# Re-placing the state-space table steps and the spatial gate's loads in a hand-written schedule

## The reference, cut to what matters

```
h = rms_norm(x, pre_g);  a_u, a_v, a_g, b_x, b_g, x_q, x_g, gates = split(h @ w_in)
y_a = a_u * (causal w_s @ layer_norm(a_v) + b_s) * silu(a_g)          # spatial gate
y_b = s5(b_x) * silu(b_g)                                             # state space
y_x = attention(x_q, rms_norm(mem) @ wk, rms_norm(mem) @ wv) * silu(x_g)
out = x + rms_norm((sum_n sigmoid(gates_n) * (y_n @ w_branch_n)) @ w_out, post_g)
```

## Time and profile before

| what | value |
|---|---|
| median of 3 runs | 2296.23 us (2295.5 to 2297.37) |
| the profiled execution: its own time | 2300.16 us |
| its span, first to last instruction | 2298.4 us |
| mean granted clock of TensorE | 0.994 of full speed |
| PE busy | 2258.7 us, 98% |
| PE weight loads (beside PE) | 1957.5 us, 85% |
| DVE busy | 1762.1 us, 77% |
| ACT busy | 1027.1 us, 45% |
| POOL busy | 298.0 us, 13% |
| device memory | 206 GB/s over the span |

### The profile page before, as it was taken

How to read it: one execution, slowest core, us unless ns; L and a number is a source line. 1 busy time by engine, 2 the same in 40 slices (tenths; PEclk the granted TensorE clock), 3 DMA queues, 4 the chain that set the end, 5 groups by cost and what they waited for, 6 DMA issues and landing times.

```text
span 2298.4 us, 30093 instructions
## 1 busy us (share of the span) xinstructions
PE 2258.7 (98%) x12660; PEld 1957.5 (85%) x12660; DVE 1762.1 (77%) x1974; ACT 1027.1 (45%) x850; POOL 298.0 (13%) x226
## 2 busy tenths in 40 slices
PE   8999999999999999999999999899999999999998
PEld 7988888888888888888888888788888888888886
DVE  7595568657797898787766889979999968458865
ACT  5553335334444545445444435344444444544432
POOL 0002200210000000000000000045887500000000
PEclk9999999999999999999999999999999999999999
DMA  7443454347755555555555566566666687576754
GB/s 271 147 159 138 147 200 153 140 147 258 276 201 201 202 201 220 202 203 202 205 205 206 204 222 227 185 244 214 210 210 212 210 294 256 192 243 250 264 205 146
DMA packets 84230, 475.19 MB, mean 207 GB/s; under 512 B 8704, under 2 KB 8832, under 8 KB 32512
## 3 DMA queue, kind: packets, MB, share of 16 engines
q1 hardware_dynamic: 84096, 473.27, 58.1%
HBM read 450.17 MB, written 23.07 MB: 206 GB/s over the span
## 4 chain that ended last, share of the span: by engine, by line
PE 84%; DVE 11%; DMA 2%; issue 1%; ACT 1%; DVEq 0%; SPq 0%; ACTq 0%
PE acc L2180 26%; PE acc L2183 25%; PE acc L2186 25%; DVE w_lo L1263 4%; PE banks L2327 2%; PE banks L2376 1%; DMA raw<-in_w 1%; DVE a_raw L1310 1%; DVE convT L1583 1%; DVE padT L1310 1%; PE banks L2455 1%; ACT w_hi L803 1%; DMA spilled<-stage 1%; PE banks L2197 1%; DVE stats L1377 0%
## 5 line engine op out<-in xcount | busy, mean ns | idle before, releaser
L1263 DVE TENSOR_TENSOR w_lo<-raw,w_hi 128x2048 fp32r<-128x2048 f32 x394 | 912.4, 2318 | 352.7 <-ACT w_hi L803 349.7
L803 ACT ACTIVATE w_hi<-raw 128x2048 fp32r<-128x2048 f32 x394 | 751.2, 1912 | 630.8 <-DMA raw<-in_w 630.2
L2180 PE MATMUL acc<-w_hi,a_hi 128*128 128x512 f32 x2112 | 815.1, 386 | 14.5 <-DVE w_lo L1263 9.4
L2183 PE MATMUL acc<-w_lo,a_hi 128*128 128x512 f32 x2112 | 802.7, 380 | 0.0
L2186 PE MATMUL acc<-w_hi,a_lo 128*128 128x512 f32 x2112 | 802.2, 380 | 0.0
L2180 PEld LDWEIGHTS acc<-w_hi,a_hi 128*128 128x128 f32 x2112 | 400.3, 190 | 84.7 <-issue 13.4
L2186 PEld LDWEIGHTS acc<-w_hi,a_lo 128*128 128x128 f32 x2112 | 400.4, 190 | 57.5 <-DVE a_lo L1299 0.3
L2183 PEld LDWEIGHTS acc<-w_lo,a_hi 128*128 128x128 f32 x2112 | 400.5, 190 | 54.0
L2180 PE MATMUL acc<-w_hi,b_hi 128*128 128x512 f32 x928 | 352.3, 380 | 0.0
L2183 PE MATMUL acc<-w_lo,b_hi 128*128 128x512 f32 x928 | 351.7, 379 | 0.0
L2186 PE MATMUL acc<-w_hi,b_lo 128*128 128x512 f32 x928 | 351.7, 379 | 0.0
(11 more groups left out here) (351 smaller groups left out, 1680.6 us busy)
## 6 DMA issues: line engine op xcount, KB each, us to landing
raw<-in_w SPq DMA_DIRECT2D x395, 1024.0 KB, 4.8
spilled<-stage SPq DMA_DIRECT2D x72, 256.0 KB, 5.9
gate_in<-spilled SPq DMA_DIRECT2D x20, 512.0 KB, 5.8
x_rows<-in_x SPq DMA_DIRECT2D x4, 512.0 KB, 9.1
x_rows<-in_x SPq DMA_DIRECT2D x1, 2048.0 KB, 10.3
mem_rows<-in_mem SPq DMA_DIRECT2D x2, 1024.0 KB, 5.9
spilled<-stage_b SPq DMA_DIRECT2D x8, 256.0 KB, 5.8
out<-y_rows SPq DMA_DIRECT2D x3, 512.0 KB, 2.8
```

The lines of the kernel that those rows point to most:

```text
L803: act.activation(w_hi[:, n % HIGH, :], raw[:, n % RAW, :], ACT.Copy)\
L1263: dve.tensor_tensor(w_lo[:, n % RAW, :], raw[:, n % RAW, :], w_hi[:, n % HIGH, :].bitcast(F32), ALU.subtract).then_inc(lo_split, 1)
L2180: pe.matmul(o, hi[:, tk], wh, start=first, stop=False)
L2183: pe.matmul(o, hi[:, tk], wl, start=False, stop=False)
```

## The change

It edits only `schedule()` and divides two steps. (1) `ssm_small` 0 goes from slot 242 to the start of slot 247, 1 from the end of slot 244 to place 497 (the end of slot 248). What stood in part 1 is now in four parts (1, 11, 12, 13) and what stood in part 2 in two (2, 14), one at the end of each of the slots 248 to 253, parts 3 to 10 before the split of slots 254 to 261. (2) ACT's exp, tanh and sines are a step `ssm_sin` of their own, at the start of slot 248. (3) The loads of c are issued two slots earlier, in slot 245. (4) `ssm` starts 2 slots later, with all that is placed relative to it: `load_av` is now at slot 321, and a of the cross attention is 335 and not 333. `xa_gate` is placed relative to `w2_gate2` and stays at slot 349. (5) From `load_av` on, the loads of the spatial gate are two slots apart (321, 322, 324, 326, 328), `sg_norm` stands at places 648, 650, 652, and ACT's square root (`sg_root`) at place 649, behind the split.

```diff
-    put(end("xa_wv", 1) + 2, "ssm_small", 0)
-    put(end("xa_wv", 1) + 4, "ssm_small", 1)
-    for part in range(2, 11):
-        put_at(2 * end("xa_wk", 1) - 2 + 2 * part, "ssm_small", part)
-    put(end("xa_wk", 1) - 1, "load_c")
+    at = 2 * end("xa_wk", 1) - 2
+    put_at(at + 2, "ssm_sin")
+    for place, part in ((0, 0), (3, 1), (5, 11), (7, 12), (9, 13), (11, 2), (13, 14)):
+        put_at(at + place, "ssm_small", part)
+    for part in range(3, 11):
+        put_at(at + 8 + 2 * part, "ssm_small", part)
+    put(end("xa_wk", 1) - 3, "load_c")
     a = end("w2_bx", 1) + 1
...
-        at = 2 * (a + 3) + 1 + SSM_PLACES * i
+        at = 2 * (a + 5) + 1 + SSM_PLACES * i
...
-    a += 3 + -(-SSM_PLACES * 17 // 2)
-    for i, name in enumerate(("load_av", "load_ln_gb", "load_au", "load_ag")):
-        put(a - 1 + i, name)
-    put(a + 4, "load_km")
+    a += 5 + -(-SSM_PLACES * 17 // 2)
+    for place, name in ((-1, "load_av"), (0, "load_ln_gb"), (2, "load_au"), (4, "load_ag"), (6, "load_km")):
+        put(a + place, name)
+    put_at(2 * a + 5, "sg_root")
...
             def ssm_small(part):
+                if part:
+                    return
+                act.wait_ge(pe_used, end(f"w_mlp_down{NPIECE - 1}", 3))
+                act.activation(ssm_t[:, 0, :], cols["log_dt"], ACT.Exp).then_inc(act_done, me.done("ssm.dt"))
+
+            def ssm_sin():
                 T_ = lambda i: ssm_t[:, i, :]
...
+                act.wait_ge(dve_done, me.at("ssm.ab"))
+                act.activation(T_(4), T_(1), ACT.Exp).then_inc(act_done, me.done())
+                act.activation(T_(5), T_(1), ACT.Tanh, scale=0.5).then_inc(act_done, me.done())
+                act.activation(T_(6), T_(3), ACT.Sin).then_inc(act_done, me.done())
+                act.activation(T_(7), T_(3), ACT.Sin, scale=0.5).then_inc(act_done, me.done("ssm.sin"))
...
-
-
+                if part == 11:
...
+                if part == 12:
...
+                if part == 13:
...
+                if part == 14:
...
-                if part >= 3:
+                if 3 <= part <= 10:
```

More of the change, by code:

```diff
@@ L1021, in ssm_small @@
             def ssm_small(part):
-                T_ = lambda i: ssm_t[:, i, :]
[L1023 to L1031, removed]
+                if part:
[3 more added lines that the diff above has]
+            def ssm_sin():
+                T_ = lambda i: ssm_t[:, i, :]
+                act.wait_ge(dve_done, me.at("ssm.ab"))
[3 more added lines that the diff above has]
+                act.activation(T_(7), T_(3), ACT.Sin, scale=0.5).then_inc(act_done, me.done("ssm.sin"))
             def ssm_u():
@@ L1098, in _ @@
                      "hidden_square": hidden_square,
-                     "ssm_small": ssm_small, "ssm_u": ssm_u, "ssm_gelu": ssm_gelu,
-                     "sg_norm": lambda part: root("sgn", 64, NT) if part == 0 else None,
+                     "ssm_small": ssm_small, "ssm_sin": ssm_sin, "ssm_u": ssm_u, "ssm_gelu": ssm_gelu,
+                     "sg_root": lambda: root("sgn", 64, NT),
                      "gelu_turn": gelu_turn, "plain_hi": plain_hi,
```

## The result

| kernel | us, median (lowest to highest) | runs | ratio to before, 95% |
|---|---|---|---|
| before | 2295.5 (2294.84 to 2297.37) | 5 | |
| changed | 2305.69 (2304.6 to 2306.48) | 5 | 1.0043 [1.0028, 1.0057] |
| before, beside the last experiments | 2296.88 (2293.61 to 2300.17) | 23 | |
| changed, timed again with them | 2303.93 (2301.07 to 2305.22) | 6 | 1.0029 [1.0017, 1.0041] |

The changed kernel is slower, by 10.2 us in the first timing and by 7.1 us in the second. The forecast was 2302.6 us (range 2296.5 to 2309), from +6.4 us between profiled executions. Those two took 2300.16 and 2306.13 us: +6.0.

The account below looks back on a forecast made before the run. PE, busy 98% of the span, was taken as the bound, so only its idle and lower clock count. Terms -8.4 - 1.6 + 16.4 + 0 = +6.4 us gave 2306.6 profiled, 2302.6 us at the median (range 2296.5 to 2309).

Parts of the forecast that it names:

- tables (244 to 255): Ahead of units 247 and 251: 12.6 us of idle and lower clock go, 4.2 us come at unit 250; net 8.4 won.
- gate and state space (256 to 351): Spatial gate's 1.6 us of PE waits all won; state space stage priced at nothing.
- late load (351 to the end): load_xg stuck behind unit 351, splits queued behind xa_gate: 14.2 us idle plus 2.2 us lower clock, 16.4 us lost.
- My +4.5 by that rule: Whole sum if the skill's transfer rule priced xg_rows' two loads at 4.4 us, making the late idle 1.8 us shorter.
- The new idle: PE idle ahead of unit 250, from ssm_sin ahead of ACT's split: 2.5 us, plus 1.7 us of lower clock.
- The spatial gate: Loads two slots apart and the root no longer holding a split back win 1.6 us; bound: none of it.
- The state space stage: DVE waits up to 4 us for POOL's first rotation in slot 262; price nothing, bound 2 us lost.
- The early gains: Rival one, units 244 to 255: all 14.2 us won, late stall at its lower bound; +1.2, 2297.4 us; chance 0.26.
- The load is not hidden: Denies rival two: load_xg lands early enough for unit 352's split, faster, 2286 us; chance 0.08.
- the third rival: Denser state space stage starves PE by 2 us, late load costs 17.9: +10.5, 2306.7 us; chance 0.14.

Follow-up runs that it names:

- Experiments 2 to 5: Late stall: load_xg earlier and xa_gate later (ratio 0.9967), attention later in the kernel before (1.0069), only the load earlier (0.9997), only xa_gate later (0.9986).
- experiment 2: Changed kernel with load_xg one slot earlier and xa_gate two slots later: 2287.4 us, ratio to before 0.9967.
- Experiments 9 to 11: Repaired kernel with gate loads bunched: 2284.61 us; with the old root place as well: 2284.8 us; kernel before with only the spatial gate's edits: 2296.01 us.
- the repaired kernel: Changed kernel with load_xg one slot earlier, xa_gate two slots later and ssm_sin half a slot later, behind ACT's split of unit 250: 2283.13 us, ratio 0.9943.
- run 3: Kernel before with a of the cross attention 335 instead of 333, xa_gate still at slot 349: 2311.2 us, ratio 1.0069.
- experiments 4 and 5: Changed kernel with only load_xg one slot earlier: 2295.33 us, ratio 0.9997; with only xa_gate two slots later: 2293.78 us, ratio 0.9986.

## Why the prediction held, and where it did not

The direction and the term that decides it were right; one smaller term, the step to the median that hangs on it, and one reason were not. The stretches of the trace answer to the terms of the sum:

```
                                predicted   first profiles   all profiles
tables (244 to 255)                -8.4         -8.4            -7.4
gate and state space (256 to 351)  -1.6         -1.9            -2.0
late load (351 to the end)        +16.4        +16.9           +17.0
start (to unit 243)                 0           -0.7          scatter
```

"All profiles" takes means: 73.56 us for five profiles with the old tables against 66.21 for five with the new ones and the sines in front; 551.45 (three) against 549.44 (ten); 245.28 (three) against 262.27 (four). The start ranges from 1422.2 to 1426.6 us over all 14 profiles, 1424.5 in the mean, with no order by kernel.

**The late load**, the term that decides the sign, came as worked out. Here are SP's queue in the changed kernel, beside the earlier trace rows, the landing of xg_rows, beside the earlier trace rows, and DVE, beside the earlier trace rows:

```profile
2042.86 0.90 SPq L752 DMA_DIRECT2D spilled<-stage  x2
2043.93 1.33 SPq L645 DMA_DIRECT2D xg_rows<-spilled  x2
```

```profile
DMA to landing us min/median/max: 6.8/7.1/7.3
```

```profile
1456.98 2.29 DVE L1267 TENSOR_TENSOR w_lo<-raw,w_hi 128x2048 fp32r<-128x2048 f32 x1 [4.96 <-ACT w_hi L805]
...
1536.08 1.23 DVE L1923 TENSOR_TENSOR prod<-banks,rot 128x1024 f32<-128x1024 f32 x1 [3.65 <-POOL rot L1228]
...
2052.20 2.29 DVE L2018 TENSOR_TENSOR xqT<-xqT,xg_rows 128x2048 f32<-128x2048 f32 x1 [21.69 <-DMA xg_rows<-spilled]
2054.41 6.69 DVE L1267 TENSOR_TENSOR w_lo<-raw,w_hi 128x2048 fp32r<-128x2048 f32 x3
```

From the end of unit 351 (2042.1) the store's issues end after 1.7 us, where I had 2.45; the loads land at 2052.2, 6.8 to 7.3 us after their issue, at the upper end of my 6.2 to 7.2; `xa_gate` takes 2.2 us, and PE restarts 2.44 us after the split begins. These small errors partly cancel, which is luck: 14.73 us of idle, where I took 14.2 from 13.7 to 14.7. The clock behind it costs 16.86 - 14.73 = 2.1 us (predicted 2.2). Experiments 2 to 5 show cause and shares.

The landing bears on a rule. The same two loads took 3.7 to 4.5 us in experiment 2, issued ahead of the store at a DMA share of 0.77 (2035 to 2040). They took 5.0 to 6.2 us in the kernel before, also ahead of the store, at a share of 0.94 (2036 to 2045), and 6.8 to 7.3 in the changed one, behind the store, at 0.99 (2043 to 2052). The Trainium skill, "DMA: Bandwidth & Descriptors", Anatomy of one DMA, gives 2.0 us plus bytes / 436e3 for a transfer (for GpSimd's path; these are SP's); taken as one transfer of 1 MB, the two loads would take an estimated 4.4 us by it. The trace agrees with that in the first case and not in the others. (My +4.5 by that rule starts from 6.2 us; from the 6.7 us that my 14.2 goes by, it would be +4.1.) What goes with the time here is how full the DMA engines are, more than the place against the store; no run here varied that share by itself.

**The tables.** The new idle came as worked out too: 2.53 us against 2.5. ACT's timeline answers to the earlier trace rows:

```profile
1451.62 0.20 ACT L870 ACTIVATE stats<-stats 128x2 f32<-128x2 f32 x1 [2.49 <-DVE stats L1401]
1451.84 1.28 ACT L1032 ACT_TABLE_LOAD   x1
1453.14 0.23 ACT L1032 ACTIVATE ssm_t<-ssm_t 128x32 f32<-128x32 f32 x1
1453.27 0.21 ACT L1033 ACTIVATE ssm_t<-ssm_t 128x32 f32<-128x32 f32 x1
1453.50 1.28 ACT L1034 ACT_TABLE_LOAD   x1
1454.80 0.23 ACT L1034 ACTIVATE ssm_t<-ssm_t 128x32 f32<-128x32 f32 x1
1454.93 0.21 ACT L1035 ACTIVATE ssm_t<-ssm_t 128x32 f32<-128x32 f32 x1
1455.05 5.49 ACT L805 ACTIVATE w_hi<-raw 128x2048 fp32r<-128x2048 f32 x3
```

From the root's end, 1451.82, to the split at 1455.05 are 3.23 us; I had 3.2. The idle that the change removes is there in every profile with the old tables (5.26 to 5.28 us at the first stop, 1.95 to 2.79 at the second). What the prediction had wrong here was the lower clock behind the old stops, 3.2 + 1.7 us from a single execution. The five profiles have 5.2, 2.3, 2.1, 4.9 and 4.6 us in all, so the mean is 3.8, and the term is -7.4 instead of -8.4.

The same rows show what the load of a table costs: the two at 1451.84 and 1453.50 begin 0.02 us after the instruction ahead of them ends, last 1.28 us, and the next instruction begins 0.02 us after their end. The Trainium skill, "ScalarE: Activation LUTs", What ACT_TABLE_LOAD costs, adds 1.38 us of drain to each; an estimate by it has 2.8 us more of idle, 5.3 in all. The trace has 2.53, so it does not bear the drain out here.

**The spatial gate.** Size right (-1.9 against -1.6), reason wrong. The prediction said that the spaced loads and the root behind the split win it. Experiments 9 to 11 show that neither the one nor the other does: bunched and with the old root the repaired kernel has no wait there, and the edits alone in the kernel before leave 1.2 us of idle, as much as run 3 has without them. That the size fits is luck. I had also counted 5 MB of loads within three units; the trace of the kernel before has 4.5 MB issued from 1864.4 to 1874.4, and the last 1 MB only at 1890.5. And I had treated the two-slot shift as neutral for this stage. It moves the stage's loads and steps against the ends of chunks and their stores; which of them is then out of the way was not isolated and stays open.

**The state space stage** cost nothing, as said. DVE waited for POOL's first rotation for 3.65 us (the row of 1536.08 above; up to 4 predicted), and PE's only wait between units 256 and 351 is the one for `u_rows`, which the kernel before has as well.

**From the profile to the median.** I took the 3.9 us by which before's profiled execution lay above its median off the forecast too, as if both kernels had them. Against the means of all profiles, 2.1 us of them lie before the end of unit 243 (1426.57 against 1424.5), which scatters in every kernel, and 1.4 us in units 244 to 255 (12.83 lost against 11.4), nearly all of it in the lower clock behind stops that the change takes away. The 1.4 us were counted as won and then taken off again. This is the error of the tables' term seen from the other side, not a further one. With the means of all profiles the sum is -7.4 - 2.0 + 17.0 = +7.6, and the forecast would have been 2296.23 + 7.6 = 2303.8 us. The second timing has 2303.93. Of the 3.1 us by which 2302.6 fell short of the first, 2305.69, some 1.2 are explained by this, and 1.9 stay open.

**The rivals.** The early gains were not whole (2.5 us of idle ahead of unit 250 in all five profiles). The load is not hidden, unless both it and its consumer move. The scan stage doesn't starve PE; the third rival's time of 2306.7 is close to the first median, but its mechanism is absent, and its -1.0 for the gate, where the forecast has -1.6, was given no reason.

**What is not settled.** The first timing's difference (10.2 us) is larger than the 7.6 us of the profiles' terms, the second's (7.1) is near them. The two ratios' intervals overlap, and no profile shows a further term.

## What to carry to other kernels

When a group of steps is moved in a schedule written by hand, list the ones whose places are computed from another anchor: here the load moved with `a` and its consumer stayed with the end of `w2_gate2`, and two slots turned a load that was free into 14.7 us of idle. Look for each moved load at what the issuing queue waits for at its new place; the last slot of a chunk that is stored was the bad one here, since its steps wait for the chunk's end and its store, and by then PE had no finished split left to work on. And price an idle of PE from several profiles, not one: the idle of the large stops repeated within 0.3 us (5.26 to 5.28, 14.44 to 14.75), while the loss to the lower clock behind them and the next stop ranged from 2.0 to 5.2 us.

## What the runs showed of the hardware

The granted clock behind the same stop differs between executions of the same schedule. Behind 5.26 us of idle ahead of unit 247 it was 0.54 over 7 us once and 0.69 another time; behind 2.5 us ahead of unit 250 it was 0.72 over 6 us in the changed kernel, and in the run with only `xa_gate` moved, which has the same schedule up to slot 349, it stayed at full speed:

```profile
1457.00:1463.00 6.00, 4.75 (x22) 4.21 (x23) 5.62 (x15) 4.35 (x3) 0.00 (x0) 1.00 0.39 160
```

That execution lost 0.2 us behind the idle, the four others 1.7 to 1.9. The second stop of the old tables, 1.95 to 2.79 us long, has the same two outcomes: 0.2 us in two executions and 1.8 to 1.9 in three. Nor does the loss grow with the idle: behind 14.4 to 14.8 us it was 2.0 to 2.1 us in three executions and 3.2 in one, behind 5.1 and 4.1 us (experiments 4 and 5) 3.2 and 2.7. What decides which of these an execution gets, no run here shows.
